# A fused two-block transformer layer on one core: the last down unit in two column halves, and GpSimd for one half of the output's scaling

## The reference

```python
x = x + hier_moe(h2, ...)            # top 2 experts of 32 for each token
return rmsnorm_2(x, norm_f_g)

def rmsnorm_2(x, g):
    xf = x.astype(jnp.float32)
    y = xf * lax.rsqrt(jnp.mean(xf * xf, axis=-1, keepdims=True) + NORM_EPS)
    return (y * g.astype(jnp.float32)).astype(x.dtype)

# one expert, for the rows h of the tokens that chose it (D = 1024, D_EXPERT = 256):
#   a = silu(h @ w_gate[e]) * (h @ w_up[e]);   y = a @ w_down[e]
# then each token adds gate * y
```

## Time and profile before

| | |
|---|---|
| median of 3 runs | 688.41 us (687.55 to 689.34) |
| the profiled execution's own time | 687.79 us |
| its span, first to last instruction | 686.0 us |
| TensorE busy (matmul) | 665.4 us, 97% |
| VectorE, ScalarE, GpSimd busy | 353.8, 293.3, 149.3 us |
| share of the chain that ended last | PE 87%, DMA 4%, DVE 3%, POOL 2% |
| DMA rate in the expert stage, the last quarter | about 420 GB/s |
| mean granted clock of TensorE | 0.995 of full speed |

### The profile page before, as it was taken

The page is one execution under the profiler, slowest core; times in us unless marked ns, Lnnn a source line. Parts: engine busy times, 40 slices in busy tenths (PEclk is TensorE's granted clock), DMA queues, the critical chain, the costliest instruction groups (busy, mean ns, idle before and its releaser), DMA issues.

```text
span 686.0 us, 12104 instructions
## 1 busy us (share of the span) xinstructions
PE 665.4 (97%) x4941; PEld 538.1 (78%) x4941; DVE 353.8 (52%) x574; ACT 293.3 (43%) x484; POOL 149.3 (22%) x148
## 2 busy tenths in 40 slices
PE   6999999999999999999999999999999999999994
PEld 5998886999999999987999999987555555455552
DVE  6369545666666666676556455584532322232223
ACT  5244556364444444456473534443223222322223
POOL 0597856033333333332004000000000000000000
PEclk9999999999999999999999999999999999999998
DMA  8971324655555554541554346989999999999994
GB/s 341 424 271 61 124 80 171 241 184 184 185 187 186 183 184 183 192 170 62 184 185 132 150 177 271 370 300 425 403 392 423 419 419 420 423 418 420 420 419 195
DMA packets 26257, 181.46 MB, mean 265 GB/s; under 512 B 2912, under 2 KB 3168, under 8 KB 5216
## 3 DMA queue, kind: packets, MB, share of 16 engines
q1 hardware_dynamic: 26064, 180.69, 67.5%
q10 hardware_dynamic: 144, 0.07, 0.1%
HBM read 179.70 MB, written 1.05 MB: 263 GB/s over the span
## 4 chain that ended last, share of the span: by engine, by line
PE 87%; DMA 4%; DVE 3%; POOL 2%; issue 1%; ACT 1%; POOLq 0%; SPq 0%; DVEq 0%; ACTq 0%
PE psum L708 51%; PE psum L1313 8%; PE psum L1337 4%; PE psum L1297 4%; PE psum L1320 4%; DMA small_units<-units_in 4%; PE psum L1329 4%; PE psum L695 1%; PE psum L671 1%; DVE ffn_w_low L549 1%; DVE arena L2278 1%; PE psum L1054 1%; POOL first_odd L1949 1%; DMA const<-const_in 1%; PE psum L747 1%
## 5 line engine op out<-in xcount | busy, mean ns | idle before, releaser
L549 DVE TENSOR_TENSOR ffn_w_low<-ring,ffn_w_high 128x2048 fp32r<-128x2048 f32 x55 | 131.3, 2387 | 111.0 <-ACT ffn_w_high L544 110.7
L544 ACT ACTIVATE ffn_w_high<-ring 128x2048 fp32r<-128x2048 f32 x56 | 107.5, 1919 | 141.1 <-PE psum L708 141.0
L708 PE MATMUL psum<-ht_high,ffn_w_high 128*128 128x256 f32 x552 | 156.8, 284 | 0.8 <-DVE ffn_w_low L549 0.8
L708 PE MATMUL psum<-ht_low,ffn_w_high 128*128 128x256 f32 x552 | 156.2, 283 | 0.0
L708 PE MATMUL psum<-ht_high,ffn_w_low 128*128 128x256 f32 x552 | 156.2, 283 | 0.0
L708 PEld LDWEIGHTS psum<-ht_high,ffn_w_high 128*128 128x128 f32 x552 | 105.9, 192 | 2.5 <-DVE ffn_w_low L549 1.2
L708 PEld LDWEIGHTS psum<-ht_low,ffn_w_high 128*128 128x128 f32 x552 | 105.9, 192 | 0.3
L708 PEld LDWEIGHTS psum<-ht_high,ffn_w_low 128*128 128x128 f32 x552 | 105.9, 192 | 0.0
L2594 DVE SCALAR_TENSOR_TENSOR weighted<-psum,arena,weighted 128x512 fp32r<-128x512 f32 x31 | 23.3, 751 | 66.3 <-ACT weighted L1835 66.3
L1986 POOL TENSOR_TENSOR arena<-arena 128x512 f32<-128x512 f32 x10 | 28.6, 2864 | 119.2 <-ACT arena L1682 96.9
L1813 ACT ACTIVATE arena<-psum,arena 128x512 f32<-128x512 f32 x32 | 22.0, 688 | 57.2 <-PE psum L1313 52.6
(11 more groups left out here) (399 smaller groups left out, 1236.6 us busy)
## 6 DMA issues: line engine op xcount, KB each, us to landing
ring<-units_in SPq DMA_DIRECT2D x93, 1024.0 KB, 4.9
arena<-units_in SPq DMA_DIRECT2D x33, 1024.0 KB, 16.8
spare_units<-units_in SPq DMA_DIRECT2D x10, 1024.0 KB, 16.7
small_units<-units_in SPq DMA_DIRECT2D x9, 1024.0 KB, 16.8
early_unit<-units_in SPq DMA_DIRECT2D x4, 1024.0 KB, 16.1
HN<-units_in SPq DMA_DIRECT2D x4, 1024.0 KB, 16.7
rows<-units_in SPq DMA_DIRECT2D x4, 1024.0 KB, 16.4
features_unit<-units_in SPq DMA_DIRECT2D x4, 1024.0 KB, 19.3
```

What stands on the lines that cost most here:

```text
L544: nc.scalar.activation(parts_slot(n)[0], w, ACT.Copy).then_inc(hi_ready, 1)
L549: nc.vector.tensor_tensor(l, ring[:, n % RING, :], h.bitcast(fp32), SUB).then_inc(lo_ready, 1)
L708: last = mm(o, l[a], r[b], start=start and (a, b) == pairs[0], stop=stop and (a, b) == pairs[-1])
```

## The change

The last down unit is loaded by two DMAs, one for each column half (of each of the four blocks of 512 columns in a partition, 256 columns, 1 KB), each with its own semaphore. TensorE's list takes the product of half 0, then tile 0's scatter of expert 30, the product of half 1, and tile 1's scatter. GpSimd, after both roots, scales the left half of tile 0 in HN (`first_left`), ScalarE only that of tile 1. Two pairs of semaphores far ahead, in the attention stage, become one each.

```diff
+        def in_column_halves(v, n):
+            return v.rearrange("p (a b) -> p a b", a=4)[:, :, n * 256:(n + 1) * 256]
...
-            for k in range(DEEP, len(IN_TURN)):
+            for k in range(DEEP, len(IN_TURN) - 1):
                 sp.wait_ge(unit_used, IN_TURN[k - DEEP] + 1)
                 load(IN_TURN[k])
+            sp.wait_ge(unit_used, IN_TURN[len(IN_TURN) - 1 - DEEP] + 1)
+            for n in range(2):
+                sp.dma_start(in_column_halves(slots[home_of(UNITS - 1)][:, 0:UNIT], n), in_column_halves(units_in[UNITS - 1], n)
+                             ).then_inc(last_half_loaded[n], 16)
...
-                sp.wait_ge(out_left, tt + 1)
+                if tt == 0:
+                    sp.wait_ge(first_left, 1)
+                else:
+                    sp.wait_ge(out_left, 1)
                 sp.dma_start(out[tt, :, left], HN[:, tt, left]).then_inc(out_stored, 16)
...
-            pe.wait_ge(qmt_sb, 1)
-            pe.wait_ge(kmt_sb, 1)
+            pe.wait_ge(mla_sb, 2)
...
-            pe.wait_ge(fq_sb, 1)
-            pe.wait_ge(fk_sb, 1)
+            pe.wait_ge(f_rows_sb, 2)
...
-            w = unit(pe, down_of(last_e))
+            w = slots[home_of(down_of(last_e))]
             pe.wait_ge(ae_ready, EXPERTS)
-            for n in range(2):
-                expert_down(w, (n, n), n * 256, 256).then_inc(last_down, 1)
+            pe.wait_ge(last_half_loaded[0], 16)
+            expert_down(w, (0, 0), 0, 256).then_inc(last_down, 1)
             pe.wait_ge(y_lo, EXPERTS - 1)
-            for tt in range(TT):
-                last = scatter((last_e - 1) % 2, tt, 4 + 2 * tt)
+            last = scatter((last_e - 1) % 2, 0, 4)
+            pe.wait_ge(last_half_loaded[1], 16)
+            expert_down(w, (1, 1), 256, 256).then_inc(last_down, 1)
+            last = scatter((last_e - 1) % 2, 1, 6)
             last.then_inc(scattered, 1)
...
-            for tt in range(TT):
-                act.wait_ge(rstd_ready, roots_before(FINAL + tt + 1))
-                nc.scalar.activation(HN[:, tt, 0:LEFT], HN[:, tt, 0:LEFT], ACT.Copy, scale=rstd[:, FINAL + tt, 0:1]
-                                     ).then_inc(out_left, 1)
+            act.wait_ge(rstd_ready, roots_before(FINAL + 2))
+            nc.scalar.activation(HN[:, 1, 0:LEFT], HN[:, 1, 0:LEFT], ACT.Copy, scale=rstd[:, FINAL + 1, 0:1]
+                                 ).then_inc(out_left, 1)
...
+            pool.wait_ge(rstd_ready, roots_before(FINAL + 2))
+            pool.wait_ge(last_rows, TT)
+            nc.gpsimd.tensor_scalar(HN[:, 0, 0:LEFT], HN[:, 0, 0:LEFT], rstd[:, FINAL, 0:1], None, MUL
+                                    ).then_inc(first_left, 1)
```

More of the change, by code:

```diff
@@ L427, in build @@
         evac_dve, evac_act = sem("evac_dve"), sem("evac_act")
[L428 to L431, removed]
+        lat_hn, lat_tr, lat_ct, lat_up, q_split, qk_rot, qk_tr, mla_sb = map(
+            sem, ("lat_hn", "lat_tr", "lat_ct", "lat_up", "q_split", "qk_rot", "qk_tr", "mla_sb"))
+        fz_ready, flog_ready, flf_ready, ft_sb, f_rows_sb, fox_pads = map(
+            sem, ("fz_ready", "flog_ready", "flf_ready", "ft_sb", "f_rows_sb", "fox_pads"))
         group_tr, gt_dve, gt_act = map(sem, ("group_tr", "gt_dve", "gt_act"))
@@ L459, in build @@
         last_down, last_hi, last_lo = sem("last_down"), sem("last_hi"), sem("last_lo")
+        last_half_loaded = [sem(f"last_half_loaded{i}") for i in range(2)]
+        first_left = sem("first_left")
         more_done, more_back, last_rows, out_right, out_left, out_stored = map(
@@ L495, in loads_of @@
             return loaded_ahead[home_of(n)] + sum(home_of(m) == home_of(n) for m in range(U_EXP, n + 1))
+        def in_column_halves(v, n):
+            return v.rearrange("p (a b) -> p a b", a=4)[:, :, n * 256:(n + 1) * 256]
+        assert home_of(UNITS - 1) != HALVES
         def arrived(n):
@@ L1602, in _ @@
                 last = copy(QF[HD:HD + 1, f, :], FT[32 * f:32 * f + 1, :])
-            last.then_inc(fq_sb, 1)
+            last.then_inc(f_rows_sb, 1)
             exps(4)
@@ L1623, in _ @@
                             psum[0:MLA_QK, 6 + tt, :].rearrange("p (h n) -> p h n", h=MLA_HEADS))
-            last.then_inc(kmt_sb, 1)
+            last.then_inc(mla_sb, 1)
             group_scale(2)
@@ L2200, in _ @@
                 last = V_.tensor_copy(KF[FOX_K - 1:FOX_K, f, :], FT[32 * f:32 * f + 1, :])
-            last.then_inc(fk_sb, 1)
+            last.then_inc(f_rows_sb, 1)
             def take_latents(tt):
@@ L2239, in _ @@
                                       psum[0:MLA_QK, tt, :].rearrange("p (h n) -> p h n", h=MLA_HEADS))
-            last.then_inc(qmt_sb, 1)
+            last.then_inc(mla_sb, 1)
             group_scale(2)
```

## The result

| | |
|---|---|
| the kernel before, same chip | 687.64 us median (686.78 to 689.34, 19 runs) |
| the changed kernel | 690.11 us median (689.16 to 694.44, 19 runs) |
| ratio | 1.0036, 95% interval 1.0028 to 1.0044 |
| its profiled execution | 690.82 us, span 689.0 us |

The change makes the kernel 2.5 us slower (1.9 to 3.0 by the interval), 0.36%: inside the predicted range of 688.1 to 690.6, but past the 0.3% that the prediction called no change, and three times its sum of 0.85 us. That the absolute time lies in the range is partly luck: the range was built on a kernel before of 688.41 us, the median of three runs, and the 19 runs beside the changed kernel gave 687.64. The measured ratio on 688.41 would be 690.9 us, outside.

What follows compares the result with a forecast made beforehand. The expert stage was taken to end on a full DMA queue, then a tail of some 10 us of engine hand-overs. Order 0.45 plus stores 0.40, loads and semaphores 0, on 688.41 gave 689.3 us (+0.12%), range 688.1 to 690.6.

Steps and rivals of the forecast that it cites:

- sum of 0.85 us: Whole change: 0.45 us later from the order on TensorE plus 0.40 us from the stores behind GpSimd's scaling.
- GpSimd's scaling: Final norm: GpSimd takes 0.64 us for tile 0's left half, tile 1's stores wait behind its store, 0.4 us later.
- GpSimd over 1.3 us: Sign in the changed kernel's profile that the forecast is wrong: GpSimd's scaling of tile 0's left half taking longer than 1.3 us.
- left 1 moves by GpSimd's time less 0.25: SyncE's stores: tile 1's left half is issued later by GpSimd's scaling time less 0.25 us; 0.4 us at 0.64.
- Rival B: Final norm: GpSimd's scaling is slow, 2.9 us; 691.5 us in all, past 0.3% from 1.9 us on; chance 0.07.
- The order on TensorE: Expert tail: half 1's product waits behind low results and a scatter, ends 677.36 not 676.73; y_done 0.45 us later.
- The two loads: Last down unit's load: 1 KB pieces make half 1 land 0.4 us later, hidden with 0.6 us to spare.
- Rival A: Last down unit's load: 1 KB pieces are slow, 5.8 us in place of 2.9; 691.1 us in all; chance 0.08.
- Semaphores: Merged pairs far ahead take two waits off TensorE: 0, at most 0.1 us gained.
- Rival C: Expert tail: half 1's chain decides, 0.43 us earlier, but the stores' 0.4 us eat it; 688.4 us; chance 0.10.
- within 0.3%: Whole kernel: time changes by less than 2.07 us, called no change; chance 0.86.
- 0.11 for slower: Whole kernel: chance 0.11 of being slower by over 0.3%, from most of A and B, the rivals of slow pieces and slow GpSimd.

Runs made afterwards that it cites:

- e2: Kernel before, with only GpSimd scaling tile 0's left half after both roots, its store still second: 689.55 us, ratio 1.0025 (1.0016 to 1.0035).
- e5: Kernel before with GpSimd scaling tile 0's left half, but that half's store last on SyncE's queue: 689.06 us, ratio 1.0008 (0.9998 to 1.0019).
- e6: Kernel before plus GpSimd scalar-column products and copies after the last store, alone and beside VectorE: product 1570 ns, copy 614 ns on 128x512; total time not meaningful.
- e1: Changed kernel, but ScalarE scales both left halves as before: 689.13 us, ratio 1.0017 (1.0008 to 1.0025) to the kernel before.
- e3: Kernel before with only TensorE's order changed as in the change, whole load: 688.92 us, ratio 1.0019 (1.0007 to 1.0032).
- e11: Same kernel as e3, repeated in another group: 688.79 us, ratio 1.0018 (1.0007 to 1.0029).
- e4: Kernel before with only the load split in column halves, each product waiting for its half, order as before: 687.51 us, ratio 0.9993 (0.9982 to 1.0004).
- e9: Same kernel as e4, repeated in another group: 688.31 us, ratio 1.0004 (0.9995 to 1.0012).
- e8: Kernel before, unchanged, measured again: 687.81 us, ratio 0.9997 (0.9988 to 1.0006).
- e10: Kernel before, whole load, with half 1's product behind both tiles' scatters of expert 30: 689.25 us, ratio 1.0022 (1.0012 to 1.0032).
- e7: Kernel before with only the two pairs of semaphores merged: 688.43 us, ratio 1.0006 (0.9997 to 1.0016).

## Why the prediction was right in kind and short in size

*GpSimd's scaling: the term that failed.* The prediction took **0.64 us**, the cast with a little for the scalar, "since one tensor input is what both have". The instruction takes 1.59 us (changed kernel, e2, e5) and 1.57 in e6, 2.6 times the copy: the number of tensor inputs was the wrong mark of likeness. It lies beyond the 0.6 to 1.3 us on which the range was built, and by the prediction's own sign ("GpSimd over 1.3 us") its account of this term is wrong. The formula beside it ("left 1 moves by GpSimd's time less 0.25") held: 1.59 - 0.25 = 1.34 us against 1.38 measured. So this term was +0.40 and is +1.38 in the trace; e2's ratio gives 1.7 us (1.1 to 2.4) in time.

The trace of the kernel before had a better row between the two that were read. The product with two inputs stands there twice, on two lines that multiply the same operands (GpSimd's lines by source; ns min/median/max):

```profile
L1986 POOL TENSOR_TENSOR arena<-arena x10: 1298/3206/3207, 142.1 to 292.9; 128x512 f32<-128x512 f32 x10
...
L1987 POOL TENSOR_TENSOR af_high<-arena x10: 1291/1292/3352, 144.2 to 294.1; 128x512 fp32r<-128x512 f32 x10
```

The mean of 2,864 ns mixes instructions of 1.3 and of 3.2 us; what makes the long ones long isn't shown. At 1.3 us the prediction's own formula gives +1.05 us, a sum of 1.5 us.

Rival B had the right place and direction, and its price of 2.9 us was too high. That the measured ratio is past 0.3% at 1.59 us, where B was to pass it at 1.9, isn't GpSimd's doing alone, but comes from the rest of the time that the sum below leaves open.

*The order on TensorE: right mechanism, size about right.* From the mark to the end of half 1's product it was 676.73 - 674.62 = 2.11 us and is 678.46 - 675.64 = 2.82, so 0.7 us more, forecast 0.63; to the first square it is 0.49 us more, forecast 0.45. What the prediction didn't say is that this price isn't fixed. The new order gives 4.48 or 4.49 us in all four profiles (changed kernel, e1, e3, e11), because VectorE's low results set it: the scatter starts 1.52 or 1.53 us after the mark. The old order depends on when the unit lands: its interval is the start of the products against the mark plus 2.95. For the kernel before that start is 1.04 after the mark, hence 3.99; e6 (0.82) had 3.79, e2 (1.34) 4.29, e5 (1.35) 4.32. In e4 and e9 the start is 0.35, and with the 0.23 us for the wait between the halves the rule gives their 3.53. So for the changed kernel, whose half 0 is in early, the price is about 0.2 us where the unit is late and 0.9 where it is early. Over the nine profiles with a whole load (before, e2, e3, e5 to e8, e10, e11: 1.04, 1.34, 0.67, 1.35, 0.82, 1.17, 1.34, 0.67, 0.75) the mean start is 1.02 after the mark, so its mean price is about 0.5, as an estimate.

With a whole load (e3, e11) the new order suffers from a late unit too, since the scatter can't start before 0.57 us after half 0's product (676.44 - 675.87 in e4). Its price therefore doesn't sink under 0.58 us (4.49 - 2.95 - 0.96, where 0.96 = 1.53 - 0.57 is the start from which on the scatter is held up), and over the same nine starts its mean is 0.7, again an estimate. The ratios of e3 and e11 give 1.2 to 1.3 us, from 0.5 up by their intervals, and the differences of the medians 0.9 and 0.8: the tail explains the better part. What the rest is, if it is anything, stays open; e9, whose tail interval is 0.4 shorter than the rule's mean and whose time isn't, leaves a gap of the same kind.

*The two loads: hidden, as forecast.* Forecast was 0.4 us late, with 0.6 to spare. Half 1 landed at 676.6 where it was wanted at 677.8. Rival A is refuted: the unit took 2.8 us behind its forerunner, not 5.8. The fixed cost for each transfer that the Trainium skill gives ("DMA: Bandwidth & Descriptors", "Anatomy of one DMA"), there for transfers issued from GpSimd, doesn't show in this full queue on SyncE, as the prediction had argued from the spacing.

*Semaphores.* Forecast was 0, and at most 0.1 us gained. e7 shows no difference; its interval goes from 0.2 us faster to 1.1 slower. *Rival C, a gain:* no. Its condition, tile 0's scatter through before half 1 lands, wasn't met: half 1 was in at 676.6, before that scatter even began (677.16). And e4 and e9 show that even the shortest tail gives no clear gain.

*The sum.* With the measured GpSimd time the prediction's own steps give 0.45 + 1.34 = 1.8 us, against 2.5 (1.9 to 3.0) measured. The experiments alone give 1.2 (e1) + 1.7 (e2) = 2.9, each give or take 0.6 to 0.7. The rest, some 0.7 us, is of the size by which the order's ratios exceed their trace, and is left open. The chance of 0.86 for "within 0.3%" rested on a GpSimd time that wasn't in the trace and whose upper bound in the profile, 2.9 us, was over four times the value taken; 0.11 for slower was too little for that.

## What to carry to other kernels

A price taken from a similar instruction needs the same operation and operand forms, not only the same shape and the same count of tensors; where the profile has none, give the bounds real weight, and look at the spread of a group before its mean is taken as a price. Work moved to an idle engine is off the path only if nothing is queued behind its result: with an in-order queue of stores, what finishes last has to stand last. Splitting a product so that one half fills idle time, while the other half goes behind a wait, pays only if the consumers of that other half aren't the longer chain.

## What the runs showed of the hardware that was not expected

GpSimd's product with a scalar column costs 1570 ns on 128x512 float32 (e6) where its copy costs 614, and more than the 1292 ns that the product of two tensors mostly takes in the kernel before.

TensorE's granted clock fell to about half, its level of 1.2 GHz, in the tail of two profiled executions whose programs in the tail are those of before (e7, e8). Busy time by windows of 2 us, e8 (length; busy us and counts of PE, PEld, DVE, ACT, POOL; granted clock, as a share of the full 2.4 GHz; DMA share; GB/s):

```profile
674.00:676.00 2.00, 1.07 (x8) 0.16 (x8) 0.48 (x2) 0.61 (x2) 0.00 (x0) 1.00 0.49 201
676.00:678.00 2.00, 1.26 (x12) 0.59 (x16) 1.01 (x2) 0.13 (x2) 0.00 (x0) 0.54 0.05 20
678.00:680.00 2.00, 2.00 (x14) 1.16 (x8) 0.97 (x2) 0.90 (x2) 0.00 (x0) 0.50 0.00 0
```

And the products of the last unit there:

```profile
676.74 1.94 PE L1329 MATMUL psum<-small_units,arena 128*32 128x256 f32 x16 [1.41 <-DMA small_units<-units_in]
```

They took 1.94 us, 1.07 at full clock, and the first square came 6.6 us after the mark. Ahead of the fall TensorE was idle for 1.41 us; but e2 and e5 waited 1.40 and 1.41 us there and stayed at full clock, so the wait alone doesn't decide it. This execution of e8 took 691.28 us, 3.5 over its kernel's median, that of e7 689.50, 1.1 over.

The last unit lands late in some executions, with 8 KB pieces too. First rows of the chains of waits of e2 and of e5 (start, us from issue to landing):

```profile
649.40 26.70 DMA small_units<-units_in
```

```profile
650.28 26.39 DMA small_units<-units_in
```

In the kernel before it was 25.68, in e3 25.2 (650.17 to 675.4). At the end of two late landings the DMA share is that of one of the 16 engines: 0.07 in e2 from 674.5 to 676.0, 0.06 in e8 from 676.5 to 677.5. The 1.02 us by which the changed kernel's tail began late are twice the order's term: a single pair of profiles (here +3.0 us) can't be read as the change, only stretch by stretch from a mark near the edit.
